# Stick-breaking attention on one Trainium2 core: the tiles of a head pair in the order 0, 7, 1, 6, 2, 5, 3, 4 in place of 0 to 7

## What is computed

```python
for blk in range(S // Q_BLOCK):            # 8 query tiles of 128 rows
    start = blk * Q_BLOCK; end = start + Q_BLOCK
    kb, vb = k[:, :end], v[:, :end]        # tile blk reads blk + 1 blocks of 128 keys
    z = einsum('bqhd,bkhd->bhqk', q[:, start:end], kb) * scale
    log_1m = where(strict, log_sigmoid(-z), 0.0)
    between = cumsum(log_1m, axis=3, reverse=True) - log_1m
    w = where(strict, exp(log_sigmoid(z) + between), 0.0)
    outs.append(einsum('bhqk,bkhd->bqhd', w, vb))
```

## Time and profile before

| | |
|---|---|
| median of 3 executions | 2149.9 us (2147.8 to 2150.7) |
| the profiled execution, its time | 2150.6 us |
| its span in the profile | 2148.8 us |
| mean granted PE clock | 0.962 of 2.4 GHz |
| PE busy over the span | 94% |
| DVE, ACT, POOL busy | 73%, 65%, 21% |

### The profile page before, as it was taken

One profiled execution on the slowest core, in us unless ns is written; L12 is line 12 of the kernel. 1 busy time (PEld: TensorE's weight loads), 2 busy tenths in 40 slices (PEclk: granted clock), 3 DMA queues, 4 the chain that ended last, 5 costly groups with the idle time before them and its releaser, 6 DMA issues.

```text
span 2148.8 us, 37954 instructions
## 1 busy us (share of the span) xinstructions
PE 2024.3 (94%) x11367; PEld 1578.8 (73%) x11368; DVE 1562.0 (73%) x1941; ACT 1395.1 (65%) x1879; POOL 460.5 (21%) x625
## 2 busy tenths in 40 slices
PE   6999999879894999999999999999999999999997
PEld 4778777767773788877787777777876778576583
DVE  4566566556666799988897787887886788685595
ACT  4566667554332688887786676776775677485483
POOL 2222112444542121111111111111111111021022
PEclk9999999869996999999999999999999999999996
DMA  6101011031125899999999898998997899696695
GB/s 220 40 20 30 20 36 44 1 127 60 55 77 179 324 358 379 368 379 358 317 375 309 287 344 283 348 360 285 329 352 251 291 338 339 241 352 238 221 318 188
DMA packets 249540, 507.23 MB, mean 236 GB/s; under 512 B 44470, under 2 KB 61676, under 8 KB 249228
## 3 DMA queue, kind: packets, MB, share of 16 engines
q1 hardware_dynamic: 233852, 462.99, 60.6%
q0 software_dynamic: 15632, 43.53, 7.9%
HBM read 471.83 MB, written 38.55 MB: 238 GB/s over the span
## 4 chain that ended last, share of the span: by engine, by line
PE 78%; DVE 6%; SPq 6%; ACT 5%; issue 3%; DMA 2%; POOL 0%; ACTq 0%; POOLq 0%; DVEq 0%
PE bank L1098 29%; PE bank L1120 15%; PE bank L871 8%; PE bank L1132 7%; SPq L508 3%; PE bank L1149 3%; PE bank L971 2%; PE bank L952 2%; SPq L519 2%; PE bank L899 1%; PE bank L1088 1%; PE bank L1215 1%; PE bank L1066 1%; PE bank L1104 1%; DVE tB L1662 1%
## 5 line engine op out<-in xcount | busy, mean ns | idle before, releaser
L1925 DVE TENSOR_TENSOR w_low<-gu_w,w_high 128x1024 fp32r<-128x1024 f32 x528 | 618.5, 1221 | 222.0 <-ACT w_high L1465 212.8
L1465 ACT CAST w_high<-gu_w 128x1024 fp32r<-128x1024 f32 x528 | 537.7, 1052 | 239.3 <-PE bank L1120 124.0
L1098 PE MATMUL bank<-w_high,x_high 128*128 128x512 f32 x1056 | 415.9, 394 | 2.0 <-DVE w_low L1925 2.0
L1098 PE MATMUL bank<-w_high,x_low 128*128 128x512 f32 x1056 | 413.6, 392 | 0.0
L1098 PE MATMUL bank<-w_low,x_high 128*128 128x512 f32 x1056 | 412.9, 391 | 0.0
L1925 DVE TENSOR_TENSOR w_low<-dn_w,w_high 128x1024 fp32r<-128x1024 f32 x264 | 315.7, 1227 | 24.1 <-ACT w_high L1465 19.4
L1465 ACT CAST w_high<-dn_w 128x1024 fp32r<-128x1024 f32 x264 | 270.1, 1050 | 24.9 <-PE bank L1098 19.5
L1098 PEld LDWEIGHTS bank<-w_high,x_high 128*128 128x128 f32 x1056 | 198.8, 188 | 45.3 <-DVE w_low L1925 2.7
L1098 PEld LDWEIGHTS bank<-w_high,x_low 128*128 128x128 f32 x1056 | 198.6, 188 | 42.7
L1098 PEld LDWEIGHTS bank<-w_low,x_high 128*128 128x128 f32 x1056 | 198.8, 188 | 41.8
L1120 PE MATMUL bank<-w_high,act_high 128*128 128x512 f32 x528 | 215.6, 408 | 0.0
(11 more groups left out here) (240 smaller groups left out, 3208.3 us busy)
## 6 DMA issues: line engine op xcount, KB each, us to landing
gu_w<-in_w_gate_up SPq DMA_DIRECT2D x528, 512.0 KB, 10.7
dn_w<-in_w_down SPq DMA_DIRECT2D x132, 1024.0 KB, 14.3
w_st<-in_w_in SPq DMA_DIRECT2D x14, 512.0 KB, 3.8
xt<-in_x SPq DMA_DIRECT2D x8, 512.0 KB, 10.3
wo_sb<-in_w_out SPq DMA_DIRECT2D x2, 2048.0 KB, 10.3
x<-in_x SPq DMA_DIRECT2D x8, 512.0 KB, 4.2
residual_rows<-x SPq DMA_DIRECT2D x8, 512.0 KB, 2.6
h_rows<-h SPq DMA_DIRECT2D x8, 512.0 KB, 2.9
```

The costliest lines, as they stand in the source:

```text
L1098: mm = pe.matmul(bank[:, 2 * h + g, :], a[:, k, :], b, start=False, stop=last)
L1465: act.copy(w_high[:, u % RING, :], src).then_inc(high_ready, 1)
L1925: dve.tensor_tensor(w_low[:, u % RING, :], raw, w_high[:, u % RING, :], ALU.subtract).then_inc(split_ready, 1)
```

## The change

The tiles of each pair are taken in the order 0, 7, 1, 6, 2, 5, 3, 4, so the units of a pair have 1, 1, 8, 8, 2, 2, 7, 7, 3, 3, 6, 6, 4, 4, 5, 5 blocks. The shares of the projection are worked out with `blocks(q)` of the new order by the same rule. The banks, `prev` and the reach of the scores are worked out by the same code, and get other values. Three places that took the position of a unit for its tile are adapted: POOL's wait for the projected queries now stands ahead of each tile instead of each half of the tiles, the wait of the final norm counts by the position of the tile, and `keep_out` writes to the tile that the unit has.

```diff
+TILES = (0, 7, 1, 6, 2, 5, 3, 4)
...
-        units = [(i, 2 * p + a, "sb") for p in range(PAIRS) for i in range(NT) for a in range(2)]
+        units = [(i, 2 * p + a, "sb") for p in range(PAIRS) for i in TILES for a in range(2)]
...
-                whole = sum(q // 2 + 1 for q in part)
-                so_far = sum(q // 2 + 1 for q in part if q <= j)
+                whole = sum(blocks(q) for q in part)
+                so_far = sum(blocks(q) for q in part if q <= j)
...
-                if i % 4 == 0 and a == 0:
+                if a == 0:
                     pool.wait_ge(proj_done, 2 * ORDER.index(p) + i // 4 + 1)
...
-                    act.wait_ge(o_kept, SB // 2 - NT + i + 1)
+                    act.wait_ge(o_kept, SB // 2 - NT + TILES.index(i) + 1)
...
             def keep_out(j):
                 dve.wait_ge(o_done, 2 * j + 2)
-                p, i = j // NT, j % NT
+                p, i = j // NT, units[2 * j][0]
                 dve.tensor_copy(o_sb[:, i, P * p:P * p + P], bank[:, 6, 0:P]).then_inc(o_kept, 1)
```

## The result

The changed kernel takes 2198.6 us (median of 4 runs, 2195.0 to 2200.5) against 2148.9 us before (4 runs). The ratio is 1.0229, with a 95% interval of 1.0217 to 1.0241: slower by 50 us. The forecast was 2200, and started from 2149.9, the median of the first three executions of the kernel before.

The account below looks back on a forecast made before the run. The prediction took PE, in its hand-written order, to bound the attention stage. 2149.9 us plus 40 us of added waits plus 10 us of clock loss gave 2200 us, with a range of 2172 to 2225 at a chance of 0.80.

Parts of the forecast that it names:

- The sum: Whole kernel: 40 us of added PE waits plus 10 us of clock loss, giving 2200 us.
- The bank waits: Full attention: PE's scores wait for DVE's last reading of their PSUM bank, 15 times for four, some 50 us for 5.0.
- The races: At each bank wait, ACT plus DVE against PE from one fill's end; PE stands 6.4, 4.05, 3.3, 1.55 us.
- Turns of values: Steps 11 and 12 of a pair: PE still waits for ACT's copy, 1.9 and 1.5 us; no gain.
- Kept tiles: PE's waits for kept tiles in a pair go: 0.8 us less.
- The last pair: Pair 3 of the attention: waits about 11.3 us against 7.7, so +3.6; window about 90 us.
- The clock: PE's granted clock falls further under longer waits in the attention: +10 us, bounded between +0 and +24.
- The upper bound: Clock loss grows with the waiting, 17.7 us for 29 us of waits: 40 us more waits lose 24 more.
- my count: Each wait of 2 us or more brings a slow stretch, about 2.2 us each; about 14 such stretches make +13.
- A sign of being wrong: Forecast would be wrong if, among other signs, DVE is found waiting for PE instead; no size given.
- Faster by mixing: Rival: alternating short and long tiles evens out the attention's load, -10 us, about 2140 us; chance 0.07.
- No change: Rival: PE's waits only move, longer bank waits eating what turns of values and slow clock cost; 2150 us, chance 0.03.

Follow-up runs that it names:

- e1: Changed kernel, with PE reaching ahead only for scores whose bank was last held by the current unit or an earlier one: 2163.5 us.
- e11: Changed kernel with blocked scores issued behind the next step's fill, kept-tile copy ahead of the stick, turns of projected values behind the fill: 2114.5 us.
- e12: Kernel before (old order and dealing) with late blocked scores, kept-tile copy ahead of the stick, turns of projected values behind the fill: 2116.2 us.
- e14: Repeat of e11 (new order, all three moves) on another chip: 2117.7 us, 0.9867 of before.
- e15: Repeat of e12 (old order, all three moves) on the same chip as e14: 2115.6 us, 0.9852 of before.
- e9: Kernel before with only the turns of projected values put behind the fill of their step: 2151.8 us.
- e13: Changed kernel with only DVE's copy of a finished tile put ahead of the stick: 2213.7 us.
- e10: Changed kernel with blocked scores issued behind the next step's fill and DVE's copy of a finished tile ahead of the stick: 2126.1 us.
- e5: Kernel before with a PE wait for DVE's last reading of the next unit added ahead of three fills per pair: 2193.8 us.
- e2: Changed kernel with the blocked narrow unit's scores issued behind the fill of the next step: 2153.5 us.

## Why the prediction was right, point by point

- **The sum.** Forecast +50, measured +50, but the parts say that some of this is luck: the waits came to +35.7 us for +40.2, the clock in the stage to +9.9 for +10, and the medians are 5 us further apart than the two profiles in which these parts were read.
- **The bound.** PE in its written order. The stage grew by 45.6 us, all else shrank by 1.2.
- **The bank waits.** Forecast 15 and some 50 us; measured 15 and 50.1. The races add up to 54 us in fact. In a middle pair 6.4, 4.05, 3.3 and 1.55 us were forecast, 5.5 (5.9 in the third pair), 3.6, 3.05 and 1.3 measured, each lower by 0.2 to 0.9. At the first of them ACT and DVE took 11.55 us for 11.7, PE 6.0 for 5.3: PE's path was priced short. In the first pair the wait was 6.1 for 5.6. The whole idle time grew by 35.7 us for +40.2.
- **Turns of values.** Forecast 1.9 and 1.5 us, measured 1.88 and 1.40. Kept tiles cost PE under 1 us, as said. But I took that wait for gone, when it was only in the shadow (e1).
- **The last pair** was the step that failed. I had it at about 90 us with 11.3 us of waits. It took 83.1 with 5.49, 0.53, 0.69, 2.56 and 0.63 us at its larger gaps, 10.2 with the small ones, where the kernel before stands 8.4. The larger part of the miss is its clock, 0.94 for 0.92: it was at half for 10.2 us in place of 13.7, and 3.9 of them lie in the wait of 5.49 us, so the clock took 3.6 us less than before where I expected more. Of the four turns that I let come late, two did, by 0.24 and 0.53 us.
- **The clock.** +10 forecast, +9.9 by the balance of the stage, which two errors made to fit. The first three pairs are 47.3 us longer with 33.9 us more of idle time, so their clock took 13.4 us; the last one took 3.6 less than before. The upper bound, lost clock in proportion to the waits (+24), was too much, since part of the slow time lies in the gaps.
- **The rule on the clock.** In the changed kernel the clock fell during each of the ten waits of 3 us and more, or within 0.2 us of its end. With the short ones my count, that each wait of 2 us or more brings a slow stretch, doesn't decide (below). The rule that the prediction takes from the Trainium skill, page "TensorE: Matmul & The Clock Gate", section "HAM oscillation — how this bites in real kernels", that long idle stretches bring the clock down each time anew, agrees with the trace for these ten. The 13 us of loss that I estimated by it are too low: 53 us at half lie outside the gaps, which at half their length is 27 us.
- **A sign of being wrong** was that DVE would be found waiting for PE instead. It does wait more, 35.5 us for 6.3 at the sum from the right, but beside PE's own waits and not in their place.
- **Rivals.** Faster by mixing: the runs e11, e12, e14 and e15 show the mixing itself to be worth nothing. No change: the waits moved in e9 as that rival said, but not in the change, where they were added.

## What to carry to other kernels

When buffers of two sizes share a ring, list for every request who held its place last: where a small one follows a large one, a fixed reach-ahead asks for it too early, and on an in-order queue everything behind it stands too. Put such a request behind work that doesn't need it. A wait taken away shows the next one on the same chain (e1, e9), and the same repair can cost 15 us or bring 27 depending on which wait still stands (e13, e10): follow the chain to its end before pricing a move.

## What the runs showed of the hardware that I had not expected

A wait of PE can cost more than its length. The 37.1 us of added waits in e5 cost 46 us, since the granted clock falls to its half level at them (0.91 over the stage for 0.95), and taking 27.6 us of idle time out of e2 (38.0 to 10.4 in e11) brought 39. Half-clock time that falls into idle time is free: 34 us more of half clock cost only 9.9 us in the changed kernel, as 15 us lay in PE's gaps.

A wait of about 2 us may or may not bring the clock down. Behind one of 2.02 us in the last pair of the kernel before, the window reads:

```profile
382.00:386.00 4.00, 4.00 (x16) 3.50 (x17) 3.30 (x3) 0.86 (x2) 0.09 (x1) 0.50 0.00 0
```

And behind one of 2.54 us in e11:

```profile
335.90:339.00 3.10, 3.10 (x27) 3.01 (x27) 1.88 (x4) 2.75 (x7) 0.21 (x1) 1.00 0.00 0
```

In the stage of the kernel before, all six waits of 2 us or more were followed by half clock; neither of the two in e11 was, nor of the two between 2 and 3 us in the changed kernel (2.00 and 2.56). Over the stages of all fourteen traces, half clock began in or up to 2.6 us behind 33 of 45 waits of 2 to 3 us, and in or within 0.2 us of all 54 of 3 us and more.
